# Where the layer loops of ScalarE and VectorE begin and end, and when the last tile is turned

## What is computed

```python
for l in range(DEPTH):                     # DEPTH = 2
    h = rmsnorm(x, pre_g[l])
    proj = jnp.einsum('bsd,de->bse', h, w_in[l])          # 1024 -> 2816
    u_a, v_a, g_a, q, k, v, g_b = jnp.split(proj, idx, axis=-1)
    y_a = gmlp_group(u_a, v_a, ...) * jax.nn.silu(g_a)
    y_b = gqa_axial_attention(q, k, v, ...) * jax.nn.silu(g_b)
    out = jnp.einsum('bse,ed->bsd', jnp.concatenate([y_a, y_b], axis=-1), w_out[l])
    x = x + rmsnorm(out, post_g[l])
```

```python
h = jnp.concatenate([pad, meta, x], axis=1)
xn = rms_norm(h, norm_gain[l])
proj = xn @ w_in[l]
```

## Time and profile before

| | |
|---|---|
| median of 3 runs | 997.31 us (997.17 to 997.38) |
| profiled execution | 997.09 us, span 995.2 us |
| TensorE busy | 975.6 us (98% of the span) |
| VectorE, ScalarE, GpSimd busy | 628.6, 499.2, 257.9 us |
| granted TensorE clock | 0.998 of full speed |

### The profile page before, as it was taken

The page is one execution under the profiler, slowest core; times in us unless marked ns, Lnnn a source line. Parts: engine busy times, 40 slices in busy tenths (PEclk is TensorE's granted clock), DMA queues, the critical chain, the costliest instruction groups (busy, mean ns, idle before and its releaser), DMA issues.

```text
span 995.2 us, 13842 instructions
## 1 busy us (share of the span) xinstructions
PE 975.6 (98%) x5030; PEld 826.6 (83%) x5030; DVE 628.6 (63%) x917; ACT 499.2 (50%) x891; POOL 257.9 (26%) x202
## 2 busy tenths in 40 slices
PE   7999999999999999999999999999999999999997
PEld 6988888888888888888788888988888887888886
DVE  5677678928777777938435586589556985312214
ACT  5444656525435655624448577433556984222222
POOL 2216100003126200003231031031224876134231
PEclk9999999999999999999999999999999999999999
DMA  9332201231432201232422011122220112323312
GB/s 293 113 108 82 68 22 43 85 130 51 134 107 78 91 22 43 81 116 53 149 85 85 1 43 43 43 85 85 85 85 22 42 34 74 107 85 106 126 44 84
DMA packets 66791, 80.46 MB, mean 81 GB/s; under 512 B 5520, under 2 KB 50704, under 8 KB 66720
## 3 DMA queue, kind: packets, MB, share of 16 engines
q1 hardware_dynamic: 64816, 76.64, 24.2%
q10 hardware_dynamic: 1904, 2.88, 0.8%
HBM read 77.42 MB, written 2.10 MB: 80 GB/s over the span
## 4 chain that ended last, share of the span: by engine, by line
PE 62%; issue 28%; DVE 4%; POOL 3%; ACT 2%; DMA 1%; POOLq 0%; ACTq 0%; DVEq 0%
PE ps L1881 16%; PE ps L1883 16%; PE ps L1882 16%; PE ps L1938 1%; PE ps L1936 1%; PE ps L1937 1%; PE ps L2223 1%; PE ps L2341 1%; PE ps L2356 1%; POOL small L549 1%; DMA x<-in_x 1%; PE ps L2369 1%; PE ps L2229 1%; PE ps L2371 1%; PE ps L2209 1%
## 5 line engine op out<-in xcount | busy, mean ns | idle before, releaser
L594 POOL TENSOR_TENSOR wlo<-raw,whi 128x2048 fp32r<-128x2048 f32 (+1 forms) x24 | 105.8, 4408 | 261.5 <-ACT whi L927 261.5
L1881 PE MATMUL ps<-whi,hhi 128*128 128x512 f32 (+1 forms) x320 | 115.8, 362 | 2.1 <-DVE hlo L1231 1.3
L1883 PE MATMUL ps<-whi,hlo 128*128 128x512 f32 (+1 forms) x320 | 114.5, 358 | 0.0
L1882 PE MATMUL ps<-wlo,hhi 128*128 128x512 f32 (+1 forms) x320 | 114.4, 357 | 0.0
L1881 PE MATMUL ps<-hhi,whi 128*128 128x512 f32 x288 | 113.1, 393 | 0.0
L1882 PE MATMUL ps<-hlo,whi 128*128 128x512 f32 x288 | 112.3, 390 | 0.0
L1883 PE MATMUL ps<-hhi,wlo 128*128 128x512 f32 x288 | 112.2, 390 | 0.0
L927 ACT ACTIVATE whi<-raw 128x2048 fp32r<-128x2048 f32 (+1 forms) x33 | 60.6, 1836 | 87.0 <-PE ps L1883 86.8
L693 ACT ACTIVATE whi<-raw 128x2048 fp32r<-128x2048 f32 (+1 forms) x29 | 52.2, 1798 | 73.0 <-PE ps L1883 73.0
L1240 DVE TENSOR_TENSOR wlo<-raw,whi 128x2048 fp32r<-128x2048 f32 (+1 forms) x29 | 63.5, 2190 | 39.4 <-ACT whi L693 38.0
L1936 PE MATMUL ps<-hhi,whi 128*128 128x512 f32 x192 | 76.8, 400 | 0.0
(11 more groups left out here) (320 smaller groups left out, 2355.0 us busy)
## 6 DMA issues: line engine op xcount, KB each, us to landing
raw<-in_w_in SPq DMA_DIRECT2D x42, 1024.0 KB, 5.3
raw<-in_w_out SPq DMA_DIRECT2D x12, 1024.0 KB, 5.0
raw<-in_w_in SPq DMA_DIRECT2D x10, 512.0 KB, 4.1
raw<-in_w_branch_swa SPq DMA_DIRECT2D x4, 1024.0 KB, 4.9
raw<-in_w_branch_sb SPq DMA_DIRECT2D x4, 512.0 KB, 3.5
x<-in_x ACTq DMA_DIRECT2D x3, 512.0 KB, 6.6
out<-x SPq DMA_DIRECT2D x3, 512.0 KB, 2.6
ws<-in_spatial_w SPq DMA_DIRECT2D x2, 512.0 KB, 7.1
```

The costliest lines, as they stand in the source:

```text
L594: pool.tensor_tensor(wlo[s][:, 0:n, :], raw[s][:, 0:n, :], whi[s][:, 0:n, :].bitcast(F32), ALU.subtract).then_inc(slab_split, 1)
L1881: pe.matmul(out_ap, lhsT=lhi(k), rhs=rhi(k), start=first and k == 0, stop=False, skip_group_check=True)
L1882: pe.matmul(out_ap, lhsT=lhi(k), rhs=rlo(k), start=False, stop=False, skip_group_check=True)
L1883: m = pe.matmul(out_ap, lhsT=llo(k), rhs=rhi(k), start=False, stop=last and k == n - 1, skip_group_check=True)
```

## The change

**Loops.** ScalarE's loop now begins with the sums of squares of tiles 2 and 3 and the copies of tile 2, so the jump back stands behind the last sum of squares of the output projection (`sum_out(1, 3)`). VectorE's loop now ends behind `hlo` of tile 3. **Tile 3** is turned in the middle of unit (0,2), behind its first 6 matmuls, in both blocks. **Meta rows:** in the second block the transposes of the meta row stand behind unit (0,3) instead of ahead of it, and `meta_values(0)` behind (1,2) instead of behind (0,3), so slab 0 is read for one unit longer and the entry of slab 2 goes from 7 to 8. **End:** for the last tile GpSimd adds the small constant to the first half's sum ahead of time, which leaves one addition less behind the second half's.

```diff
-TILE_AT = {3: 2, 4: 3}
+TILE_AT = {3: 2}
+LAST_TILE_AT = 4
...
-UNITS_BY_SLAB2 = [7, 10, 13, 15, 17, 21, 22, 24, 29, 33, 37, 41, 45] + [47 + 2 * i for i in range(20)] + \
+UNITS_BY_SLAB2 = [8, 10, 13, 15, 17, 21, 22, 24, 29, 33, 37, 41, 45] + [47 + 2 * i for i in range(20)] + \
...
             for t in range(NT):
+                if t == 3:
+                    pool.wait_ge(fin_sq, 4)
+                    first = small2[:, 16:17]
+                    pool.tensor_tensor(first, first, eps_tile[:, 0:1], ALU.add).then_inc(last_sum, 1)
+                    pool.wait_ge(last_sum, 1)
                 pool.wait_ge(fin_sq, t + 1 + t // 3)
                 m = small2[:, 8 + t:9 + t]
-                if t == 3:
-                    pool.tensor_tensor(m, m, small2[:, 16:17], ALU.add).then_inc(last_sum, 1)
-                    pool.wait_ge(last_sum, 1)
-                pool.tensor_tensor(m, m, eps_tile[:, 0:1], ALU.add).then_inc(pool_step, 1)
+                pool.tensor_tensor(m, m, small2[:, 16:17] if t == 3 else eps_tile[:, 0:1], ALU.add)\
+                    .then_inc(pool_step, 1)
...
-            for t in (2, 3):
-                act.wait_ge(x_loaded[t], 16)
-                sum_x(0, 0, t)
-            transposed_x(0, 0, 2)
             with act.Fori(0, DEPTH) as l:
+                for t in (2, 3):
+                    act.wait_ge(x_loaded[t], 16)
+                    act.wait_ge(x_back, l * 4 + t + 1)
+                    sum_x(l, 0, t)
+                transposed_x(l, 0, 2)
                 transposed_x(l, 0, 3)
...
                 sum_out(1, 3)
-                sum_next(2)
-                sum_next(3)
-                transposed_x(l, 1, 2)
...
             act.wait_ge(meta_sq, 1)
+            for t in (2, 3):
+                act.wait_ge(x_back, DEPTH * 4 + t + 1)
+                sum_x(DEPTH, 0, t)
+            transposed_x(DEPTH, 0, 2)
             transposed_x(DEPTH, 0, 3)
...
             transposed_x(0, 0, 2)
+            transposed_x(0, 0, 3)
             with dve.Fori(0, DEPTH) as l:
-                transposed_x(l, 0, 3)
...
                 transposed_x(l, 1, 2)
+                transposed_x(l, 1, 3)
                 a["chain"].append(count[0] - FIRST)
...
-            transposed_x(DEPTH, 0, 3)
...
-                def by_token_half(i, half, t):
+                def by_token_half(i, half, t, turned_between=None):
...
                     for at_ in (0, 2):
+                        if at_ and turned_between is not None:
+                            x_transposed(l, 0, turned_between)
...
-                    by_token_half(i, i, t)
+                    by_token_half(i, i, t, 3 if n == LAST_TILE_AT else None)
...
+                tokens_half(j, j, t, 3 if n == LAST_TILE_AT else None)
                 if (j, t) == (0, 3):
...
-                tokens_half(j, j, t)
-                if t == 3:
-                    if j == 0:
-                        pe.wait_ge(hm_ready, 1)
-                    meta_values(j)
+                if (j, t) == (1, 2):
+                    pe.wait_ge(hm_ready, 1)
+                    meta_values(0)
+                if (j, t) == (1, 3):
+                    meta_values(1)
```

More of the change, by code:

```diff
@@ L944, in _ @@
             for t in range(NT):
-                unit(TILE_UNITS[t] + (t >= 2))
+                unit(TILE_UNITS[t] + (t == 3))
                 copy(stacked_values(t, 0), by_pairs(ps[:, t, :])).then_inc(sv_hi, 1)
@@ L2108, in tokens, with tokens_half @@
                         lambda k: whi[s][:, k, :], lambda k: wlo[s][:, k, :], KT).then_inc(unit_done, 1)
-            def tokens_half(j, half, t):
+            def tokens_half(j, half, t, turned_between=None):
                 s, tt = j % RING, slice(t * P, t * P + P)
@@ L2115, in tokens_half @@
                 for at_ in (0, 2):
+                    if at_ and turned_between is not None:
+                        x_transposed(DEPTH, 0, turned_between)
                     if (j, t) == (0, 0):
```

## The result

The changed kernel takes 1001.60 us (median of 6 runs, 1001.14 to 1002.32), the kernel before 997.21 us (median of 6, 996.88 to 997.38): a ratio of 1.0046, 95% interval 1.0033 to 1.0059. The profiled execution took 1001.48 us with a span of 999.5 us, 4.3 us more than before's, at the same granted clock of 0.998. TensorE was busy for 976.3 us, 0.7 us more than before, so most of what was added is waiting. Two single executions of kernels further down, at 1081.52 and 5604.40 us, were slow and stand in no median.

The account below looks back on a forecast made before the run. TensorE, busy 98%, bounds the kernel, so other engines count only where it waits. Terms 2.85 + 2.3 - 0.3 = +4.85 us gave 1001.9 us from the profiled run, 1002.2 us by the median; range 999.6 to 1003.6 us.

Parts of the forecast that it names:

- ScalarE's loop: Layer 0 to 1: a 4.5 us jump delays tile 2's squares to 244.55; (0, 3) starts 1.75 us later, at 256.85.
- VectorE's loop: Layer 0 to 1: a 5.2 us jump makes slab 2's split 3.2 us late; TensorE starts slab 4 2.85 us late.
- Rival 3: ScalarE's jump costs nothing in its new place, 999.8 us; with VectorE's free too, first edge gains 0.6 us; chance 0.09.
- the first edge: Where layer 0 ends and layer 1 begins, near 238 us: whole cost forecast as +2.85 us.
- the half microsecond of waiting there: TensorE asks for slab 2 of layer 1 at 265.15; its split ends at 265.7, half a microsecond more.
- the wait for `wlo` of slab 4: In layer 1, TensorE waits for VectorE's late split and starts slab 4 2.85 us late.
- Rival 1: Both jumps are short, at their lower ends: the first edge costs 0.7 us, in all 1000.0 us; chance 0.10.
- Second edge: Layer 1 to second block, near 475 us: meta transposes behind (0, 3), +0.7; slab 2 waited for 1.55; +2.3 us.
- Rival 2: At the second block, slab 0's later release is hidden: +0.7 us there, in all 1000.6 us; chance 0.07.
- Start and end: Layer 0's start costs 0; at the kernel's end one GpSimd addition fewer gives -0.27 us.
- Rival 4: TensorE's waits for tile 3 at both edges, 1.13 and 0.69 us, go, and 0.27 at the end: 995.2 us; chance 0.04.
- its condition: At unit (0, 2), Rival 4 depends on `hlo` of tile 2 being ready when (1, 1) ends; no size of its own.

Follow-up runs that it names:

- The two parts alone: Kernel before with only tile 3 turned inside unit (0, 2), 997.75 us; kernel before with only the meta rows later, 998.58 us; each against 997.03 us.
- the fastest kernel: the combined kernel with VectorE written out, tile 3 turned inside (0, 2), first half of tile 2's `hlo` before tile 3's normalise, meta rows scaled earlier: 994.50 us.
- the combined kernel: Kernel before with ScalarE's loop ending behind tile 2's squares, VectorE's behind `hlo` of tile 3, and GpSimd's early addition: 996.91 us against 996.79.

## Why the prediction was right

**ScalarE's loop: right.** Forecast against measured: squares of tile 2 at 244.55 and 244.34, normalise of tile 2 at 246.65 and 246.42, of tile 3 at 251.15 and 250.96, (0, 2) at 253.1 and 252.90, (0, 3) at 256.85 and 256.68. ScalarE's idle time before the squares was 4.07 us, where 4.4 were expected. Three experiments (the loop alone, the jump in idle time, ScalarE written out) show that the jump is the cause. Rival 3, a free jump in its new place, is refuted by the 4.07 us.

**VectorE's loop: the term was too big.** I put 5.2 us on its jump, from before's 249.05 to 254.35. Counted the same way, from the end of ScalarE's copies (255.05 + 1.09) to the gains at 260.78, it took 4.64. The split of slab 2 came at 262.80, 2.6 us late and not 3.2, and I carried this lateness undiminished to slab 4. But before's VectorE had an idle time in front of slab 3's split, which I had overlooked:

```profile
270.22 2.29 DVE L1240 TENSOR_TENSOR wlo<-raw,whi 128x2048 fp32r<-128x2048 f32 x1 [0.51 <-DVE tok L1315]
```

It took up 0.4 us; slab 4's split ended at 289.33, 2.2 us late, and TensorE, itself 1.88 us later, did not wait for it. So the first edge cost 1.7 us, not 2.85; the steps up to slab 2 (TensorE there at 265.15, as forecast) held, but the half microsecond of waiting there and the wait for `wlo` of slab 4, one of the signs that were named, did not come, and this last step, 1.1 us, failed. The whole came to 4.4 us by the medians against 4.85, closer than this step, partly by luck: some 0.2 us at the start, put at 0, and 0.2 us scattered behind 498 us, which were in no sum, made up for part of it. The range had been drawn to shorter jumps and would have held without them. Rival 1, with short jumps and 0.7 us at the first edge, is about as far from the 1.7 us measured there as my 2.85.

**Second edge: right.** Forecast 2.3, measured 2.34: (0, 3) at 1.95 us behind its old place (1.88 of it brought along), the meta transposes behind it, slab 2 waited for 1.40 us (1.55 forecast). The two parts alone cost 0.72 and 1.55 us by their medians, 2.27 together. Rival 2, a hidden release, is refuted. What I had missed is that moving VectorE's loop end also makes the meta row late, which showed only with the meta rows back in their place.

**Start and end.** The first matmul came 0.17 us later than before and tile 1's transposes 0.22 us; the forecast had 0. The end gave 0.2 of the 0.27 us forecast. It was not run alone.

**Rival 4 (faster)** failed for the reason given for it, and its condition, once met, gave the fastest kernel, together with a VectorE without a jump.

**Open.** All kernels whose VectorE loop was changed start tile 1's transposes at 12.11 to 12.38 us, the others between 11.90 and 12.13; whether this is the order of code or the spread of x's landing was not separated. It is as large as most single gains here, and takes more than half of what VectorE's loop alone had gained up to slab 2.

## What to carry to other kernels

A loop's jump costs its engine microseconds, and where the loop ends decides who pays: put the jump where that engine is idle longer than that and the DMA queues are quiet, or write the layers out on that engine. Before a piece of work is moved out of a wait that it fills, first remove the wait: the turn inside (0, 2) alone lost 0.7 us here, and with half of a low part made ahead of a normalise the two (and the meta row's earlier scaling) won 1.3 us. When a buffer is held for one step longer, follow the slab that takes its place to its slowest producer (4.6 us on GpSimd) and compare with the time at which it is asked for.

## What was not expected of the hardware

The length of a jump depends on other transfers: VectorE's idle time at the same jump was 5.71 us with the DMA engines at a share of 0.77, 3.81 us at 0.53, and 2.48 us at 0.01. The share alone does not give the length: counted from the end of ScalarE's last copy to the next instruction, it was 6.54 us in the combined kernel at a share of 0.83, but 5.30 us in the kernel before at 1.10 (transfers overlap). What is shown is a jump of 3.31 us by this count with quiet queues against 4.6 us and more beside the loads; what sets the length between these was not found. Code of twice the length showed no stall of its own at the edges on ScalarE (0.23 us) or TensorE, whose "issue" wait near 238 us went away with its jump; VectorE's showed the 0.3 us at slab 2.
